# Layers written out, and the context tile's attention taken two head units at a time: one change to a two-layer fused transformer trunk

## The chip, the cores and the metric

The kernel runs on one core of a Trainium2 chip, as one launch. The time is device microseconds of that core, from the first to the last instruction of the program. The profiled execution is read through its profile page and through views of its trace; times inside it are microseconds from the start of the span unless marked ns.

## The reference

One inference step of a two-layer backbone over 256 latent tokens and 128 context tokens, which go through the kernel together as three tiles of 128 tokens: tiles 0 and 1 are latent, tile 2 is the context. Each layer normalises, projects, runs four mixers in parallel (A a bidirectional mLSTM, B neighbourhood attention, C sliding-window attention with a sink, D differential attention), gates and merges them, and then runs a grouped mixture of experts.

```python
for l in range(DEPTH):                                   # DEPTH = 2
    h = rmsnorm(x) * (1 + sc1) + sh1
    aq, ak, av, ao, ..., bq, bk, bv, cq, ck, cv, dq, dk, dv, gt = split(h @ w_in)
    # latent tokens attend latent keys (masked, biased) and cached context keys, in one softmax;
    # context tokens attend the 128 context keys only:
    s = einsum('bqhgd,bkhd->bhgqk', qx, k) * scale       # C: a sink logit joins the softmax
    p = softmax(s)                                       # D: p[:, :, 0] - lam * p[:, :, 1]
    y = einsum('bhgqk,bkhd->bqhgd', p, v)
    out = sum(sigmoid(gates) * (branches @ w_branch)) @ w_out
    x = x + g1 * out
    x = x + g2 * hier_moe(rmsnorm(x) * (1 + sc2) + sh2)
```

## The kernel before, in words

Every engine runs its own hand-written program, and semaphores join them. The body of a layer stands once in each engine's program, inside a hardware loop over the two layers (`Fori(0, DEPTH)`, L659 for SyncE, L790 for GpSimd, L944 for ScalarE, L1306 for TensorE, L1833 for VectorE). Since the layer number `l` is a register there, the number that a semaphore is waited for (`Signal.value`: layer times the count per layer, plus a constant) has to be worked out by register instructions. The expert part has a further hardware loop over its six tiles inside.

The order of work is one list, `SCHEDULE` (L109 to L214), that each engine walks. Its backbone is a row of GEMM units `("gemm", g)`: weights of 128x1024 numbers arrive in a ring `raw`, ScalarE rounds them to `whi`, GpSimd or VectorE subtracts to get `wlo`, and TensorE multiplies in three passes (`whi*hhi`, `wlo*hhi`, `whi*hlo`, L1328 to L1330) into the accumulator G: 18 products of 512 columns for a unit over the three token tiles. Other steps are put between units (`put`), or inside one, ahead of its second or third token tile (`put_inside`).

Attention is a pipeline of units `AU` (L91): (mixer, token tile, pair of heads). Each of the mixers B, C and D has 12 units, eight for the latent tiles and four for the context tile. Slot i of a mixer holds four steps: `sn` of unit i-1 (VectorE: reciprocal and scaling of the exponentials `prob`), `pv` of unit i-3 (TensorE: L1668 or L1671, probabilities by values into O; ScalarE and VectorE take O away as `bhi` and `blo`), `pt` of unit i-2 (TensorE transposes `prob` into T, L1641; ScalarE and VectorE copy it to `probT`), and `sc` of unit i (TensorE: scores into S, L1627, L1628 for latent tiles, L1630 for the context; VectorE: maximum, L2133; ScalarE: exponentials, L1171). Slots 0 to 8 stand after a GEMM unit each; slots 9 to 14, which hold most of the context tile's steps, stand half a unit apart:

```python
            if i < 9:
                put(g + i, *at)
            elif i % 2:
                put_inside(g + 9 + (i - 9) // 2, 1, *at)
            else:
                put(g + 9 + (i - 9) // 2, *at)
        return g + 12
```

The transposes of the next mixer's queries and keys (`tp`, L1546) use the same banks T0 and T1 as `pt` and are put inside units ahead of the third token tile. In the order rows below, `waits` lists the semaphores an instruction waits for: `pa_act` and `pb_dve` are the copies of the turned probabilities, `pn_dve` the scaled probabilities, `ol_dve` the values taken from O, `ex_act` the exponentials, `lo_done` a split weight unit, `ev_act` and `ev_dve` a GEMM tile taken out of G, `last_pe` and `sq_act` the end and the start of a layer.

Of the kernel before, what the change touches and what calls it, by code (L numbers as in the profile page):

```python
# [28 lines left out]
P = 128  # L29
D = 1024  # L30
# [60 lines left out]
AU = [(ty, t, j) for ty in "BCD" for t in range(TILES) for j in range(4)]  # L91
# [17 lines left out]
def schedule():  # L109
# [32 lines left out]
    def attention(g, first):  # L142
        for i in range(12 + 3):
            at = []
            if 1 <= i < 13:
# [3 lines left out]
            if 2 <= i < 14:  # L149
                at.append(("pt", first + i - 2))  # L150
            if i < 12:
# [17 lines left out]
    g = attention(g, 12)  # L169
# [3 lines left out]
    g = attention(g, 24)  # L173
# [25 lines left out]
    for g in range(NG):  # L199
# [3 lines left out]
        for t in range(1, TILES):  # L203
# [6 lines left out]
            (s[0] in ("sc", "sn", "pt", "pv") and s[1] >= 24)]  # L210
# [72 lines left out]
def program(nc, a, out, counts):  # L283

    ctx = ExitStack()
    with ctx:
# [73 lines left out]
        am = sb("am", [P, 2, 16])  # L360
# [286 lines left out]
        def _(sp):  # L647
# [11 lines left out]
            with sp.Fori(0, DEPTH) as l:  # L659
# [120 lines left out]
        def _(pool):  # L780
# [9 lines left out]
            with pool.Fori(0, DEPTH) as l:  # L790
# [144 lines left out]
        def _(act):  # L935
# [8 lines left out]
            with act.Fori(0, DEPTH) as l:  # L944
# [46 lines left out]
                for s in SCHEDULE:  # L991
# [109 lines left out]
                    elif s == ("dma", "gate1"):  # L1101
                        need(g_out, 0)
                        need(pv_pe, 23)
# [60 lines left out]
                    elif s[0] == "sc":  # L1164
# [3 lines left out]
                        w = 384 if t < 2 else 128  # L1168
                        for m in range(2):
                            src = prob[:, u % 2, m, 0:w] if u in BIASED else S[:, m, 0:w]  # L1170
                            e = nc.scalar.activation(prob[:, u % 2, m, 0:w], src, ACT.Exp,  # L1171
                                                     bias=am[:, u % 2, m:m + 1], accum_out=am[:, u % 2, 2 + m:3 + m])
                        if ty == "C":
                            e = nc.scalar.activation(am[:, u % 2, 6:8], am[:, u % 2, 4:6], ACT.Exp)
# [6 lines left out]
                        if u in (11, 23):  # L1181
                            act.wait_ge(*sc_pe.at(l, u))
                            load_keys(u // 12 + 1)
                    elif s[0] == "pt":
                        u = s[1]
                        w = 384 if AU[u][1] < 2 else 128
                        act.wait_ge(*pt_pe.at(l, u))
                        pa_act.of(nc.scalar.activation(probT[:, u % 2, 0, 0:w], T[:, 0, 0:w], ACT.Copy))
                    elif s[0] == "pv":
# [3 lines left out]
                        if ty == "D":  # L1193
                            yd_act.of(nc.scalar.activation(slot["Dq"][:, t, j * P:(j + 1) * P], O[:, 0:P], ACT.Copy))
                        else:
                            n = TYPES.index(ty)
                            if u == 12:
                                need(kv_out["B"], 1)
                                act.wait_ge(*rope_dve.at(l, 8))
                            oh_act.of(nc.scalar.activation(bhi[n][:, j, t * P:(t + 1) * P], O[:, 0:P], ACT.Copy))  # L1200
                        if u in (11, 23):
                            load_vals(u // 12 + 1)
# [76 lines left out]
        def _(pe):  # L1279
# [26 lines left out]
            with pe.Fori(0, DEPTH) as l:  # L1306
# [62 lines left out]
                for s in SCHEDULE:  # L1369
# [87 lines left out]
                    elif s[0] in ("gemm", "rest"):  # L1457
# [5 lines left out]
                        if i == 0 and kind == "branch":  # L1463
                            need(*((tl_dve, 3), (ol_dve, 11), (ol_dve, 23), (tl_dve, 7))[arg[0]])
# [149 lines left out]
                    elif s[0] == "sc":  # L1614
                        u = s[1]
                        ty, t, j = AU[u]
                        kj = j // 2 if ty == "C" else j
                        i = "BCD".index(ty)
                        need(tp_act, max(TP_NO[ty, "q", j], TP_NO[ty, "k", kj]))
                        if u % 12 == 0:  # L1620
                            need(keys_in, i)
                        free("S0", "S1")
                        for m in range(2):
                            r = slice(64 * m, 64 * m + 64)
                            q = qT[r, j, t * P:(t + 1) * P]
# [3 lines left out]
                            else:  # L1629
                                mm = nc.tensor.matmul(S[:, m, 0:128], q, kT[r, kj, 256:384], start=True, stop=True)  # L1630
                        sc_pe.of(mm)
                        read["S0"] = read["S1"] = (sa_dve, BIASED.index(u)) if u in BIASED else (ex_act, u)
                    elif s[0] == "pt":
# [5 lines left out]
                        for m in range(maps):  # L1639
                            for b in range(3 if t < 2 else 1):  # L1640
# [6 lines left out]
                    elif s[0] == "pv":  # L1647
# [5 lines left out]
                        if u % 12 == 0:  # L1653
                            need(vals_in, "BCD".index(ty))
                        free("O")
                        blocks = [0, 1, None] if t < 2 else [2]
# [6 lines left out]
                        for i, b in enumerate(blocks):  # L1663
# [764 lines left out]
```

## Time and profile before

| | |
|---|---|
| runs of the kernel before | 1719.42, 1721.44, 1723.40 us; median 1721.44 |
| the profiled execution | 1721.81 us, its span 1720.2 us |
| TensorE busy | 97% of the span |
| VectorE, ScalarE, GpSimd busy | 60%, 51%, 38% |
| mean granted TensorE clock | 0.995 |
| HBM | 341.71 MB read, 23.93 MB written |

The span is the time from the first to the last instruction; 1.6 us of the execution's time lie outside of it. A busy TensorE is not TensorE at its peak, since the ends of its products are modelled and they overlap; the loading of weights (PEld in the rows) shows more sharply when the array takes the next piece of work.

### The profile page before, as it was taken

To read this page: it belongs to the slowest core of one execution; us is meant where nothing else is said; L and a number is where in the kernel's file an instruction comes from. 1 tells how busy PE (TensorE), PEld (TensorE's weight loads), DVE (VectorE), ACT (ScalarE), POOL (GpSimd) and SP (SyncE) were. 2 spreads that over 40 slices of the span, in tenths; PEclk is the share of its full clock that TensorE was granted. 3 is DMA by queue.
4 is the path that set the end of the run, shared out by engine and by line. 5 is a ranking of instruction groups with operands and counts; after the bars stand their busy time and mean duration, and the time that the engine had idled before them with its cause. 6 is when DMAs were issued, how large, how long until landed. Compare 5 with 4: busy or idle time off the path is not lost.

```text
span 1720.2 us, 30904 instructions
## 1 busy us (share of the span) xinstructions
PE 1666.3 (97%) x10021; PEld 1332.3 (77%) x10021; DVE 1030.5 (60%) x1820; ACT 875.4 (51%) x1499; POOL 657.9 (38%) x414
## 2 busy tenths in 40 slices
PE   6999999999999999999989999999999999999997
PEld 5788787777888877777768888777778887777775
DVE  2226567564451179999860374775635413899997
ACT  2443344445443347788744334454445334587884
POOL 0545464334467621111125454543345775101102
PEclk8999999999999999999999999999999999999999
DMA  8833343254456559999965234334354653999994
GB/s 302 289 101 106 106 147 124 96 178 141 178 195 230 184 183 397 376 369 368 323 226 195 91 112 140 117 117 141 124 184 160 214 201 138 343 383 366 376 363 159
DMA packets 120849, 367.49 MB, mean 214 GB/s; under 512 B 11964, under 2 KB 34044, under 8 KB 120704
## 3 DMA queue, kind: packets, MB, share of 16 engines
q1 hardware_dynamic: 95024, 323.99, 52.3%
q0 software_dynamic: 6624, 24.18, 3.8%
q10 hardware_dynamic: 19056, 17.52, 3.3%
q8 instruction: 75, 1.23, 0.3%
q14 instruction: 70, 0.57, 0.1%
HBM read 341.71 MB, written 23.93 MB: 213 GB/s over the span
## 4 chain that ended last, share of the span: by engine, by line
PE 57%; issue 16%; DVE 13%; POOL 6%; ACT 5%; DMA 2%; SPq 1%; ACTq 0%; DVEq 0%; POOLq 0%
PE G L1328 15%; PE G L1330 13%; PE G L1329 13%; DVE wlo L1849 4%; POOL wlo L809 4%; ACT whi L970 2%; PE T L1641 2%; PE O L1385 2%; PE S L1627 2%; PE O L1671 1%; DVE pA L1849 1%; PE S L1328 1%; DMA pC<-in_units 1%; DVE pB L1849 1%; PE S L1330 1%
## 5 line engine op out<-in xcount | busy, mean ns | idle before, releaser
L809 POOL TENSOR_TENSOR wlo<-raw,whi 128x1024 fp32r<-128x1024 f32 x198 | 489.8, 2480 | 570.8 <-ACT whi L962 570.8
L1328 PE MATMUL G<-whi,hhi 128*128 128x512 f32 (+1 forms) x1440 | 579.4, 402 | 11.4 <-DVE wlo L1849 6.8
L1330 PE MATMUL G<-whi,hlo 128*128 128x512 f32 (+1 forms) x1440 | 558.1, 388 | 0.0
L1329 PE MATMUL G<-wlo,hhi 128*128 128x512 f32 (+1 forms) x1440 | 557.9, 387 | 0.0
L1328 PEld LDWEIGHTS G<-whi,hhi 128*128 128x128 f32 x1440 | 270.8, 188 | 90.6 <-DVE wlo L1849 16.6
L1330 PEld LDWEIGHTS G<-whi,hlo 128*128 128x128 f32 x1440 | 270.9, 188 | 57.6
L1329 PEld LDWEIGHTS G<-wlo,hhi 128*128 128x128 f32 x1440 | 271.5, 189 | 46.9
L962 ACT ACTIVATE whi<-raw 128x1024 fp32r<-128x1024 f32 x204 | 214.9, 1055 | 105.8 <-PE G L1330 71.2
L1849 DVE TENSOR_TENSOR wlo<-raw,whi 128x1024 fp32r<-128x1024 f32 x150 | 179.8, 1221 | 6.3 <-ACT whi L970 3.4
L970 ACT ACTIVATE whi<-raw 128x1024 fp32r<-128x1024 f32 x144 | 152.9, 1062 | 32.3 <-PE G L1330 18.0
L970 ACT ACTIVATE whi<-pA 128x1024 fp32r<-128x1024 f32 x72 | 76.6, 1063 | 41.7 <-PE G L1330 23.3
L1849 DVE TENSOR_TENSOR wlo<-pA,whi 128x1024 fp32r<-128x1024 f32 x72 | 88.0, 1224 | 15.8 <-ACT whi L970 14.0
L1171 ACT ACTIVATE prob<-prob,am 128x384 f32<-128x384 f32 x64 | 39.1, 612 | 110.7 <-DVE am L1849 59.6
L1849 DVE TENSOR_TENSOR wlo<-pB,whi 128x1024 fp32r<-128x1024 f32 x72 | 85.2, 1223 | 6.9 <-ACT whi L970 6.3
L1328 PE MATMUL S<-whi,ehi 128*128 128x512 f32 x192 | 79.4, 413 | 6.4 <-DVE elo L1849 6.3
L970 ACT ACTIVATE whi<-pB 128x1024 fp32r<-128x1024 f32 x72 | 75.2, 1058 | 10.6 <-PE G L1330 10.3
L1328 PE MATMUL G<-whi,bhi 128*128 128x512 f32 x192 | 79.2, 412 | 0.0
L1330 PE MATMUL S<-whi,elo 128*128 128x512 f32 x192 | 75.2, 392 | 0.0
L1330 PE MATMUL G<-whi,blo 128*128 128x512 f32 x192 | 75.1, 391 | 0.0
L1329 PE MATMUL S<-wlo,ehi 128*128 128x512 f32 x192 | 75.1, 391 | 0.0
L1329 PE MATMUL G<-wlo,bhi 128*128 128x512 f32 x192 | 74.9, 390 | 0.0
L804 POOL TENSOR_TENSOR sink_col<-ones 128x1 f32<-128x1 f32 x26 | 15.3, 587 | 149.6 <-ACT yo L1264 76.6
(383 smaller groups left out, 2385.7 us busy)
## 6 DMA issues: line engine op xcount, KB each, us to landing
raw<-in_units SPq DMA_DIRECT2D x426, 512.0 KB, 4.9
pA<-in_units SPq DMA_DIRECT2D x78, 512.0 KB, 6.1
pB<-in_units SPq DMA_DIRECT2D x72, 512.0 KB, 6.3
h_sorted<-sig POOLq DMA_DIRECT2D x12, 514.0 KB, 7.5
hs<-h_sorted POOLq DMA_DIRECT2D x10, 514.0 KB, 7.8
y_sorted<-yo POOLq DMA_DIRECT2D x10, 512.0 KB, 7.0
bias<-in_nat_bias ACTq DMA_DIRECT2D x16, 256.0 KB, 3.5
kT<-in_units SPq DMA_DIRECT2D x6, 512.0 KB, 5.0
```

Of the source, the lines that this page charges most:

```text
L809: lo_done.of(nc.gpsimd.tensor_tensor(wlo[:, k, :], raw[:, POS_OF[g] % RAW, :], whi[:, k, :].bitcast(F32), ALU.subtract))
L962: hi_done.of(nc.scalar.activation(whi[:, g % CONV, :], raw[:, p % RAW, :], ACT.Copy))
L970: hi_done.of(nc.scalar.activation(whi[:, n % CONV, :], expert_raw(n), ACT.Copy))
L1171: e = nc.scalar.activation(prob[:, u % 2, m, 0:w], src, ACT.Exp, bias=am[:, u % 2, m:m + 1], accum_out=am[:, u % 2, 2 + m:3 + m])
L1328: nc.tensor.matmul(dst, st_hi, mv_hi, start=start, stop=False)
L1329: nc.tensor.matmul(dst, st_hi, mv_lo, start=False, stop=False)
L1330: return nc.tensor.matmul(dst, st_lo, mv_hi, start=False, stop=stop)
L1385: mm = nc.tensor.matmul(O[32 * q:32 * q + 32, c0:c0 + P], cond[:, k, :], raw[:, MODPOS[j - MQ + 1 + q] % RAW, k * P:(k + 1) * P], start=(k ...
L1627: nc.tensor.matmul(S[:, m, 0:256], q, kT[r, kj, 0:256], start=True, stop=True)
L1641: mm = nc.tensor.transpose(T[:, m, b * P:(b + 1) * P], prob[:, u % 2, m, b * P:(b + 1) * P], ident[:, :])
L1671: mm = nc.tensor.matmul(O[64 * m:64 * m + 64, 0:P], values(b, lo, 64), pr, **fl)
L1849: return V.tensor_tensor(o, i0, i1, op)
```

## The change

It does three things. (1) In each engine's program the loop over the layers is a Python loop, so that the body of a layer stands twice and waits are against constants; the counting pass that precedes the build walks one layer. (2) A unit of the context tile covers two pairs of heads: a mixer has `NA` = 10 units instead of 12, and the last two put side by side in one step what were two steps' scores, exponentials, transposes and products. (3) The slots of B and C stand after one GEMM unit each, 13 of them, and the last one (the last `pv`) shares its place with the first slot of the next mixer. For D the last two of 13 slots stand inside and after one unit, so that D ends where it did.

```diff
-AU = [(ty, t, j) for ty in "BCD" for t in range(TILES) for j in range(4)]
+AU = [(ty, t, j) for ty in "BCD" for t in range(TILES) for j in (range(4) if t < 2 else (0, 2))]
+NA = len(AU) // 3
...
     def attention(g, first):
-        for i in range(12 + 3):
+        for i in range(NA + 3):
...
-            if i < 9:
+            if first < 2 * NA or i < NA + 1:
                 put(g + i, *at)
-            elif i % 2:
-                put_inside(g + 9 + (i - 9) // 2, 1, *at)
+            elif i == NA + 1:
+                put_inside(g + NA + 1, 1, *at)
             else:
-                put(g + 9 + (i - 9) // 2, *at)
-        return g + 12
+                put(g + NA + 1, *at)
+        return g + NA + 2
...
+    layers = DEPTH if counts else 1
...
-            with pe.Fori(0, DEPTH) as l:
+            for l in range(layers):
...
# ScalarE, exponentials: four of 128 columns instead of two in a context unit
-                        w = 384 if t < 2 else 128
-                        for m in range(2):
-                            src = prob[:, u % 2, m, 0:w] if u in BIASED else S[:, m, 0:w]
-                            e = nc.scalar.activation(prob[:, u % 2, m, 0:w], src, ACT.Exp,
-                                                     bias=am[:, u % 2, m:m + 1], accum_out=am[:, u % 2, 2 + m:3 + m])
+                        w, n = (384, 2) if t < 2 else (P, 4)
+                        for i in range(n):
+                            m, lo = i * 2 // n, i % (n // 2) * w
+                            src = prob[:, u % 2, m, lo:lo + w] if u in BIASED else S[:, m, lo:lo + w]
+                            e = nc.scalar.activation(prob[:, u % 2, m, lo:lo + w], src, ACT.Exp,
+                                                     bias=am[:, u % 2, i:i + 1], accum_out=am[:, u % 2, 4 + i:5 + i])
...
# TensorE, scores of a context unit: both pairs of heads side by side in S
-                        for m in range(2):
+                        for o, m in ((o, m) for o in range(len(pair)) for m in range(2)):
                             r = slice(64 * m, 64 * m + 64)
-                            q = qT[r, j, t * P:(t + 1) * P]
+                            q = qT[r, pair[o], t * P:(t + 1) * P]
...
-                                mm = nc.tensor.matmul(S[:, m, 0:128], q, kT[r, kj, 256:384], start=True, stop=True)
+                                mm = nc.tensor.matmul(S[:, m, o * P:(o + 1) * P], q, kT[r, kj, 256:384], start=True, stop=True)
...
# TensorE, transposes
-                            for b in range(3 if t < 2 else 1):
+                            for b in range(3 if t < 2 else 2):
...
# VectorE, scaling of a context unit (D adds the two maps in an operation of its own)
+                        both = both.rearrange("p m (j n) -> p m j n", j=2)
+                        scaled = tt(both, both, q[:, 20:24].rearrange("p (m j) -> p m j", m=2).unsqueeze(3)
+                                    .to_broadcast([P, 2, 2, P]), ALU.mult)
+                        if ty == "D":
+                            own(scaled)
+                            scaled = tt(both[:, 0], both[:, 0], both[:, 1], ALU.add)
+                        pn_dve.of(scaled)
```

The copies and the waits of the other engines follow the new units (widths of 256 instead of 128, `NA` in place of 12). The number of products, transposes and exponentials in a layer stays; only the grouping changes.

**First place: TensorE, mixer B of a layer, a step of the context tile.** Before, the step that holds the products, transposes and scores of one context unit each:

```order
L1313 REGISTER_ALU [waits pa_act]
L1671 MATMUL O<-probT,pB 64x128 [waits ol_dve,pb_dve]
L1671 MATMUL O<-probT,pB 64x128
L1641 MATMUL T<-ident,prob 128x128 [waits pn_dve]
L1641 MATMUL T<-ident,prob 128x128
L1313 REGISTER_ALU
L1630 MATMUL S<-kT,qT 128x128 [waits ex_act]
L1630 MATMUL S<-kT,qT 128x128
L1313 REGISTER_ALU
L1328 MATMUL G<-whi,bhi 128x512 [waits ev_act]
```

Now, the step in which the last latent unit's products meet the first context unit's transposes; no scores are left for it:

```order
L1680 MATMUL O<-probT,pB 64x128 [waits ol_dve]
L1680 MATMUL O<-probT,pB 64x128 x3
L1680 MATMUL O<-probT,vc 64x128 x2
L1649 MATMUL T<-ident,prob 128x128 [waits tp_act,pn_dve]
L1649 MATMUL T<-ident,prob 128x128 x3
L1335 MATMUL G<-whi,bhi 128x512 [waits lo_done]
```

The four transposes of two units stand in one piece, the scores have gone into the two steps ahead, and no register instruction stands between the pieces.

**Second place: TensorE, from mixer B to mixer C.** Now the last products of B and the first scores of C follow each other after one GEMM unit (before, they stood one unit apart):

```order
L1680 MATMUL O<-probT,pB 64x128 [waits ol_dve,pb_dve,pa_act]
L1680 MATMUL O<-probT,pB 64x128 x3
L1635 MATMUL S<-kT,qT 128x256 [waits ex_act,keys_in]
L1636 MATMUL S<-kT,qT 128x128
L1635 MATMUL S<-kT,qT 128x256
L1636 MATMUL S<-kT,qT 128x128
L1335 MATMUL G<-whi,hhi 128x512 [waits lo_done]
```

**Third place: GpSimd, from the first layer to the second.** Before, the loop's branch goes back to the body's start:

```order
L923 TENSOR_TENSOR sink_col<-ones 128x1 [waits last_pe]
L790 REGISTER_ALU
L790 COMPARE_AND_BRANCH
```

Now the second layer's first operations (the root of the mean square of each tile) follow in the same row of instructions:

```order
L926 TENSOR_TENSOR sink_col<-ones 128x1 [waits last_pe]
L817 TENSOR_TENSOR st<-st,cval 128x1 [waits sq_act,start_dve]
L821 TENSOR_TENSOR st<-st,cval 128x1 [waits pool_ord]
L817 TENSOR_TENSOR st<-st,cval 128x1 [waits sq_act]
L821 TENSOR_TENSOR st<-st,cval 128x1 [waits pool_ord]
```

The branch is gone there, on every engine; the branches of the expert loops stay and are now built once per layer.

## Rows read from the trace of the kernel before

**Rows 1.** The page, part 1: busy time and share of each engine.

```profile
PE 1666.3 (97%) x10021; PEld 1332.3 (77%) x10021; DVE 1030.5 (60%) x1820; ACT 875.4 (51%) x1499; POOL 657.9 (38%) x414
```

**Rows 2.** Windows: stretch, PE, PEld, DVE, ACT, POOL busy (x), clock, DMA share, GB/s.

```profile
246.00:492.00 246.00, 242.35 (x1707) 188.43 (x1708) 144.47 (x316) 119.96 (x309) 102.76 (x45) 1.00 0.42 143
636.00:866.00 230.00, 224.89 (x984) 173.21 (x983) 209.03 (x262) 174.46 (x210) 29.52 (x38) 1.00 0.95 357
```

**Rows 3.** Timeline, PEld, mixer B: start, us, line, load, xcount [idle before <-releaser].

```profile
315.34 0.19 PEld L1330 LDWEIGHTS G<-whi,blo 128*128 128x128 f32 x1
315.88 0.20 PEld L1671 LDWEIGHTS O<-probT,pB 128*64 128x64 f32 x4 [0.36 <-issue]
316.25 0.20 PEld L1641 LDWEIGHTS T<-ident,prob 128*128 128x128 f32 x2 [0.17 <-issue]
316.62 0.30 PEld L1630 LDWEIGHTS S<-kT,qT 64*128 64x128 f32 x4 [0.17 <-issue]
...
317.15 0.19 PEld L1329 LDWEIGHTS G<-wlo,bhi 128*128 128x128 f32 x1
317.38 0.19 PEld L1330 LDWEIGHTS G<-whi,blo 128*128 128x128 f32 x1
```

**Rows 4.** Timeline, PEld, mixer B: three more context steps, and six transposes together.

```profile
312.16 0.19 PEld L1330 LDWEIGHTS G<-whi,hlo 128*128 128x128 f32 x1
...
314.41 0.19 PEld L1329 LDWEIGHTS G<-wlo,bhi 128*128 128x128 f32 x1
...
323.76 0.19 PEld L1330 LDWEIGHTS G<-whi,blo 128*128 128x128 f32 x1
...
324.96 0.19 PEld L1329 LDWEIGHTS G<-wlo,bhi 128*128 128x128 f32 x1
...
1146.49 0.64 PEld L1641 LDWEIGHTS T<-ident,prob 128*128 128x128 f32 x6 [0.17 <-issue]
```

**Rows 5.** Timeline, PEld: a full latent step, and the first scores of mixer C.

```profile
289.33 0.19 PEld L1330 LDWEIGHTS G<-whi,hlo 128*128 128x128 f32 x1
...
292.45 0.19 PEld L1329 LDWEIGHTS G<-wlo,hhi 128*128 128x128 f32 x1
...
332.62 0.19 PEld L1330 LDWEIGHTS G<-whi,hlo 128*128 128x128 f32 x1
...
334.12 0.19 PEld L1329 LDWEIGHTS G<-wlo,hhi 128*128 128x128 f32 x1
```

**Rows 6.** Timeline, PEld, mixer D: a context step with scores, one without.

```profile
481.17 0.19 PEld L1330 LDWEIGHTS G<-whi,blo 128*128 128x128 f32 x1
...
482.57 0.19 PEld L1329 LDWEIGHTS G<-wlo,bhi 128*128 128x128 f32 x1
...
484.87 0.19 PEld L1330 LDWEIGHTS G<-whi,blo 128*128 128x128 f32 x1
...
485.66 0.19 PEld L1329 LDWEIGHTS G<-wlo,bhi 128*128 128x128 f32 x1
```

**Rows 7.** Waits of PEld, whole span (us in total, times, longest); one VectorE operation.

```profile
PEld T L1641 <- ACT qT L1133: 3.4, 6, 1.2
PEld T L1546 <- DVE probT L2162: 2.9, 2, 1.5
...
317.33 2.41 DVE L1849 TENSOR_TENSOR prob<-prob,am 128x256 f32<-128x256 f32 x1
```

**Rows 8.** Timeline at the end of the first layer, by engine; the last is an expert-loop row.

```profile
869.83 0.19 POOL L814 TENSOR_TENSOR st<-st,cval 128x1 f32<-128x1 f32 x1 [2.66 <-issue]
...
871.71 0.95 POOL L818 TENSOR_TENSOR st<-st,cval 128x1 f32<-128x1 f32 x1
...
869.61 1.06 ACT L1007 ACTIVATE sig<-pA 128x1024 f32<-128x1024 f32 x1 [1.31 <-DVE pA L1849]
...
871.50 0.75 DVE L1930 TENSOR_SCALAR pB<-pA,st 128x1024 f32<-128x1024 f32 x1 [1.92 <-POOL st L818]
...
873.58 0.65 PE L1349 MATMUL T<-ident,pB 128*128 128x128 f32 x4 [0.94 <-DVE pB L1930]
...
713.49 1.00 ACT L1264 ACTIVATE yo<-S 128x1024 f32<-128x1024 f32 x1
```

More of the change, by code:

```diff
@@ L168, in schedule @@
     put_inside(g - 1, 2, ("tp", "C", "k", 0), ("tp", "C", "k", 1))
-    g = attention(g, 12)
+    g = attention(g, NA)
     for i in range(4):
@@ L172, in schedule @@
         put_inside(g - 1 + i // 2, 2, ("tp", "D", "k", i))
-    g = attention(g, 24)
+    g = attention(g, 2 * NA)
     put(g, ("hn", 1))
@@ L789, in _ @@
             pool.memset(dummy[:, 11:12], 0.0).then_inc(yo_free.handle, 1)
-            with pool.Fori(0, DEPTH) as l:
+            for l in range(layers):
                 chain = [0]
@@ L943, in _ @@
             act.wait_ge(cond_dve, 2)
-            with act.Fori(0, DEPTH) as l:
+            for l in range(layers):
                 chain = [0]
@@ L1305, in _ @@
             pe.wait_ge(nx_dve.handle, 1)
-            with pe.Fori(0, DEPTH) as l:
+            for l in range(layers):
                 passed = {}
@@ L1832, in _ @@
             next_cols().then_inc(nx_dve.handle, 1)
-            with dve.Fori(0, DEPTH) as l:
+            for l in range(layers):
                 chain = [0]
@@ L2147, in _ @@
                         if ty == "C":
[L2148 to L2157 removed]
+                            own(tt(q[:, 4:4 + 2 * n], q[:, 4:4 + 2 * n], q[:, 12:12 + 2 * n], ALU.add))
@@ new lines, in _ @@
+                        own(V.reciprocal(q[:, 20:20 + 2 * n], q[:, 4:4 + 2 * n]))
+                        if ty == "D" and t < 2:
+                            own(V.tensor_scalar(prob[:, u % 2, 0, 0:w], prob[:, u % 2, 0, 0:w], q[:, 20:21], None, ALU.mult),
+                                V.tensor_scalar(q[:, 21:22], q[:, 21:22], lam[:, 5:6], None, ALU.mult))
+                            pn_dve.of(V.scalar_tensor_tensor(prob[:, u % 2, 0, 0:w], prob[:, u % 2, 1, 0:w], q[:, 21:22],
+                                                             prob[:, u % 2, 0, 0:w], ALU.mult, ALU.add))
+                            continue
@@ new lines, in _ @@
+                        if ty == "D":
+                            own(V.tensor_scalar(q[:, 22:24], q[:, 22:24], lam[:, 5:6], None, ALU.mult))
+                        both = prob[:, u % 2, :, 0:n * w]
+                        if n == 1:
+                            pn_dve.of(tt(both, both, q[:, 20:22].unsqueeze(2).to_broadcast([P, 2, w]), ALU.mult))
+                            continue
+                        both = both.rearrange("p m (j n) -> p m j n", j=2)
+                        scaled = tt(both, both, q[:, 20:24].rearrange("p (m j) -> p m j", m=2).unsqueeze(3)
+                                    .to_broadcast([P, 2, 2, P]), ALU.mult)
```

104 lines of the change are left out of this document (51 added, 53 removed).

## The prediction, made before the changed kernel was timed

> **What bounds the kernel now.** I read the busy shares first: TensorE is busy 97% of the span, the next engine 60% [rows 1]. Two stretches then say which engine a saving must come from. In the three mixers B, C and D of the first layer (246 to 492 us) TensorE has 242.4 of 246 us, VectorE and ScalarE under 150, DMA a share of 0.42, and the granted clock is 1.00 [rows 2]; only what takes the array less time makes this stretch shorter. In the experts (636 to 866 us) TensorE and the DMA (0.95) are both nearly full [rows 2]; the change leaves the work there as it is. A busy share of 97% leaves about 50 us idle, but it counts changeovers of the array as busy, so the weight loads must be read one by one. Between two GEMM products the loads start 0.23 us apart (317.15 and 317.38 [rows 3]). Where attention interrupts the GEMM, I take the step's price as the first GEMM load after it, less the last before it, less two paces (0.46): the product that was still running, and the one after. This holds streaming and changeovers together, as the array feels them.
>
> **Fewer, larger pieces.** Three context steps of mixer B stand in the rows:
>
> - products, transposes and scores of one unit each: 317.15 - 315.34 - 0.46 = 1.35 us [rows 3];
> - the same with twelve products instead of four: 314.41 - 312.16 - 0.46 = 1.79, so four more cost 0.22 [rows 4];
> - products and transposes alone: 324.96 - 323.76 - 0.46 = 0.74 [rows 4].
>
> So a piece of scores costs 1.35 - 0.74 = 0.61. Its four loads make two pairs, one to each half of the array, some 0.10 us a pair, so 0.20 is streaming; the row's 0.30 [rows 3] holds the last load too, and with 0.30 the term below would be 0.1 less for each piece. The rest, 0.41, is paid once for the piece whatever its size. A transpose is 0.11 ((0.64 - 0.20) / 4, [rows 3, 4]), so products and transposes stream 0.22 + 0.22, and 0.30 of their 0.74 is paid once for the interruption. Per mixer of kind B or C the change has the scores of the context in two pieces instead of four, and 13 interruptions instead of 15: 2 x 0.41 + 2 x 0.30 = 1.42 us.
>
> In D the step with scores costs 482.57 - 481.17 - 0.46 = 0.94, and without 485.66 - 484.87 - 0.46 = 0.33 [rows 6]. Two products and one transpose stream just that, so only the scores have a changeover: 0.61 - 0.20 = 0.41, twice, 0.82 per mixer. Products and transposes there have the shape of the GEMM's tiles (128 by 128), scores do not; that fits a changeover paid per change of tile shape.
>
> A layer saves 1.42 + 1.42 + 0.82 = 3.66 us, the two layers **7.3 us**. If the changeover of pieces twice as large were to grow with their size, nothing of this would be left; against it, the twelve products cost no more per load than four. Bounds: 5.5 (0.30 of each scores piece streams: 12 pieces fewer, 1.2 us less, and some of the 2 x 0.30 kept) to 8.5.
>
> **The shared place.** B's last products and C's first scores now interrupt the GEMM once. The full latent step (twelve products, six transposes, eight scores) costs 292.45 - 289.33 - 0.46 = 2.66 [rows 5]. Products and transposes of that size are 0.74 + 0.44 + 0.44 = 1.62, so the scores add 1.04, and C's first scores by themselves cost 334.12 - 332.62 - 0.46 = 1.04 [rows 5]. Joining two steps thus saves nothing that the rows show; I take 0.
>
> **The waits of the half-spaced steps.** With two steps in one unit the transposes come before ScalarE and VectorE have cleared T. TensorE's loads wait 3.4 us in 6 waits for ScalarE's `qT` copies, and 2.9 us in 2 for VectorE's copy `probT` [rows 7]. At 317.33 VectorE's scaling of one such unit takes 2.41 us [rows 7], with the next steps due half a unit (9 x 0.23 = 2.1 us) behind. Together 6.3 us. Some of that would have passed as a changeover anyway: 0.17 at each of 8 places, the gap where nothing is waited for [rows 3], so 4.9 go at most. With whole units between the steps (18 x 0.23 = 4.1 us) these waits should go. What is late next is ScalarE: a context unit now has four exponentials in a row, ahead of the turned keys' copies, and I let 0.5 us stay. The term is **4.4 us**, bounds 0 (each wait finds another late copy) and 4.9.
>
> Queued behind TensorE's last products in the shared place are the next mixer's scores and then the GEMM. Their wait is for VectorE's and ScalarE's copies of the transposes of one unit before, some 4 us earlier; work of that kind keeps up with the full latent step at the same spacing [rows 5], so I price it at nothing. Merged copies and scalings on VectorE and ScalarE lie beside TensorE, which has over 95 us more work than either in the stretch of 246 us [rows 2]: nothing too; if that cover went, one late copy would cost about what the single waits cost now, 1.2 to 1.5 us [rows 7].
>
> **The layer boundary.** GpSimd's first operation of layer 2 starts at 869.83 after 2.66 us in which it waited for nothing that the profile shows [rows 8]; the loop's branch is in that gap. Then the root ends at 871.71 + 0.95 = 872.66 for the last tile, VectorE normalises the first tile at 871.50, and TensorE's transposes start at 873.58 [rows 8]. Written out, GpSimd still can't finish before ScalarE: its activation ends at 869.61 + 1.06 = 870.67 [rows 8], and the root follows. Its own time of 0.95 us takes the chain to about 871.6 instead of 872.7. So of the 2.66 us, **1.1 us** lie on the path and the rest hides beside ScalarE. Bounds: 0.1 and 2.7.
>
> The Trainium skill (Advanced Engine Details and Errata, Control Flow Timing) gives about 108 ns for a compare-and-branch. By that price the boundary would be worth 0.1, and the sum would be 11.8 (1710.0 us); the idle 2.66 us of the row is far over it, and the measurement decides.
>
> **Register instructions.** The order shows one ahead of the scores and none ahead of L1641, yet both gaps are 0.17 us [rows 3]. Taken as 0, with bounds 0 and 8 (first rival).
>
> **The sum.** 7.3 + 4.4 + 1.1 = 12.8, and 1721.8 - 12.8 gives **1709.0 us** against the profiled execution, which lies 0.4 above the median of the runs; I do not correct for that. The expert part and all DMA traffic carry nothing: every transfer has the same size, and starts with its own GEMM unit. A mixer's GEMM units keep their number too, and D ends at the same unit.
>
> **Rivals.**
>
> *Register work is on TensorE's path.* Then each interruption loses part of its gap of 0.36 or 0.17 us [rows 3] when the constants come in. For: no engine is named as releaser, only "issue". Against: the equal gaps with and without a register instruction. With about 0.1 us off at each of some 80 remaining places it gives 8 us more: 1701. Chance 0.12.
>
> *The waits only move.* Four exponentials in a row and the joined mixers make ScalarE's or VectorE's copies late at the one-unit spacing, and the 4.4 us come back. For: VectorE's 2.41 us operation shows that a copy can be held up by another engine [rows 7]. Against: 18 products cover 4.1 us. Then 1721.8 - 7.3 - 1.1 + 1 = 1714. Chance 0.14.
>
> *Slower: the expert loops lose their place.* They stay hardware loops, but stand twice, at other addresses; a back edge that finds its target no longer at hand would idle its engine as GpSimd does at the layer boundary. Eight more such edges (four per layer beyond the first pass, TensorE's or the slowest engine's) at 2.7 us, less 0.3 that is there now, make 8 x 2.4 = 19, less the 12.8: 1728. It decides from about five such edges on. Against: the body of one expert tile is short beside a layer's, and ScalarE's first operation after such an edge has no idle time before it (the last row of [rows 8]); the body's length does not change. Chance 0.06.
> The Trainium skill (Runtime: NRT & Kernel Launch, on instruction fetch) says that a taken branch to a target outside the prefetched window of two pages has to fetch it by DMA; GpSimd's 2.66 us agree, and straight code would be fetched ahead.
>
> *The change does not do what it says.* The order shows fewer pieces, no register instructions, and no branch at the boundary; what is left is that the gaps do not follow the pieces (changeovers grow with size), and half of the waits stay: 1721.8 - 1.1 - 2.2 = 1718.5. Chance 0.06.
>
> **How the numbers follow.** The forecast has 0.62. Its own bounds (5.5 to 8.5, 0 to 4.9, 0.1 to 2.7) do not fall together; I take 1705 to 1713 for it. The range of 1700 to 1716.5 adds the first two rivals and leaves out the last two (0.12) and the far tail of the first. About 0.2% (3.4 us) is what a measurement of this kernel can tell from no change: faster means under 1718.0, slower over 1724.9. Faster: 0.62 + 0.12 + 0.14 less a little for mishaps, 0.86; within: 0.08, mostly the last rival; slower: 0.06.
>
> **What would show it.** In the trace after: a B or C context step of eight products and four transposes costs about 0.30 + 0.44 + 0.44 = 1.18 us, one of eight products and no transposes with eight scores of C about 1.8; no wait of TensorE for `probT` or `qT` ahead of its transposes; GpSimd's first operation of layer 2 without the 2.66 us; gaps of 0.17 and 0.36 us as before. I am wrong if these gaps shrink throughout (first rival), if waits for ScalarE or VectorE appear at the one-unit spacing (second), or if the experts take more than their 230 us (third).

## The result, and the profile after

| | before | after |
|---|---|---|
| median of 6 runs each | 1719.95 us (1717.42 to 1723.4) | 1704.19 us (1700.93 to 1706.39) |
| ratio, 95% interval | | 0.9906 [0.9896, 0.9917] |
| profiled execution, span | 1720.2 us | 1704.8 us |

The kernel is faster by 0.94%, 15.8 us between the medians, where 12.8 were forecast: inside the range and under its middle. It is 0.8 us below the narrower 1705 to 1713 that the prediction gave to its own account; the profiled execution, 1706.39 us, lies inside that. The busy shares say nothing of the gain (compare [rows 1]); neither do the windows of the two stretches [rows 2], in which TensorE is as full as before. The kernel is shorter mainly because the attention stretch ends earlier. Page, part 1, and windows (stretch, PE, PEld, DVE, ACT, POOL busy, clock, DMA share, GB/s) of the kernel after:

```profile
PE 1658.0 (97%) x10021; PEld 1333.3 (78%) x10021; DVE 1014.5 (60%) x1736; ACT 871.0 (51%) x1471; POOL 657.1 (39%) x414
```

```profile
240.00:484.00 244.00, 243.28 (x1753) 193.07 (x1754) 140.62 (x275) 119.58 (x298) 108.54 (x49) 1.00 0.42 144
627.00:857.00 230.00, 224.81 (x984) 173.10 (x984) 208.96 (x262) 174.31 (x210) 28.44 (x38) 1.00 0.95 357
...
868.00:871.50 3.50, 3.50 (x8) 2.75 (x9) 2.99 (x8) 2.00 (x3) 0.00 (x0) 0.50 0.79 273
```

Both kernels load the GEMM's weights in the same order, so the start of the same load can be read in every trace, and the span falls into stretches that compare. They are, in us, from one such load to the next (start: from the span's start to the ninth GEMM unit; A: from there to the start of a unit shortly ahead of B's first scores; attention: from there to past the end of D; to the boundary: up to a load within the experts, at 800.5 us before; boundary: the last expert tiles, the turn to layer 2 and its first eight units; then the same stretches of layer 2):

| kernel | start | A | attention 1 | to the boundary | boundary | A 2 | attention 2 | rest |
|---|---|---|---|---|---|---|---|---|
| before | 81.75 | 155.24 | 263.75 | 299.74 | 123.66 | 155.17 | 264.16 | 376.8 |
| before_again | 81.53 | 155.15 | 263.63 | 299.66 | 123.89 | 155.11 | 264.18 | 376.7 |
| after | 81.12 | 154.72 | 256.29 | 299.19 | 125.59 | 154.72 | 256.71 | 376.5 |
| after_again | 79.87 | 154.72 | 256.31 | 299.40 | 124.58 | 154.72 | 257.23 | 376.5 |
| layers_only | 79.06 | 154.75 | 262.98 | 299.46 | 125.00 | 154.77 | 263.11 | 376.9 |
| attention_only | 79.39 | 155.27 | 257.75 | 299.65 | 123.97 | 155.13 | 257.01 | 376.9 |
| merged_half | 77.50 | 154.72 | 260.47 | 299.43 | 125.14 | 154.75 | 260.35 | 376.5 |
| pt_first | 79.90 | 154.77 | 256.38 | 299.42 | 125.13 | 154.71 | 257.73 | 376.5 |
| busy | 80.41 | 154.73 | 256.35 | 299.45 | 125.41 | 154.75 | 256.32 | 376.6 |
| best | 83.25 | 154.73 | 254.53 | 299.27 | 124.61 | 154.75 | 254.79 | 376.7 |
| best_busy2 | 79.95 | 154.76 | 254.83 | 299.19 | 123.52 | 154.74 | 254.70 | 376.6 |
| layers_pe | 80.16 | 155.09 | 264.16 | 299.69 | 125.41 | 155.11 | 263.83 | 377.0 |
| layers_act_dve | 82.79 | 154.79 | 262.99 | 299.21 | 125.32 | 154.81 | 262.87 | 376.7 |
| apart | 78.51 | 154.71 | 257.79 | 299.16 | 124.91 | 154.71 | 257.87 | 376.5 |

The stretches A and attention repeat within 0.6 us from trace to trace, most of them within 0.1; the start does not (77.5 to 83.3). Of the 15.4 us between the two spans, 7.5 are in each attention stretch, 0.5 in each stretch A, 0.6 in the start, 0.8 in the remainder, and the boundary gives 1.9 back.

The pieces on TensorE's loads came out as the sum had them. Timeline of the kernel after, PEld, mixer B (start, us, line, load, count, [idle before <-releaser]):

```profile
315.81 0.19 PEld L1337 LDWEIGHTS G<-whi,blo 128*128 128x128 f32 x1
316.36 0.42 PEld L1680 LDWEIGHTS O<-probT,pB 128*64 128x64 f32 x8 [0.36 <-issue]
316.75 0.25 PEld L1680 LDWEIGHTS O<-probT,vc 128*64 128x64 f32 x4
317.17 0.42 PEld L1649 LDWEIGHTS T<-ident,prob 128*128 128x128 f32 x4 [0.17 <-issue]
317.56 0.19 PEld L1335 LDWEIGHTS G<-whi,bhi 128*128 128x128 f32 x1
317.67 0.19 PEld L1336 LDWEIGHTS G<-wlo,bhi 128*128 128x128 f32 x1
...
322.02 0.19 PEld L1337 LDWEIGHTS G<-whi,blo 128*128 128x128 f32 x1
322.57 0.42 PEld L1680 LDWEIGHTS O<-probT,pB 128*64 128x64 f32 x8 [0.36 <-issue]
323.16 0.42 PEld L1649 LDWEIGHTS T<-ident,prob 128*128 128x128 f32 x4 [0.17 <-issue]
...
323.66 0.19 PEld L1336 LDWEIGHTS G<-wlo,hhi 128*128 128x128 f32 x1
...
327.34 0.19 PEld L1337 LDWEIGHTS G<-whi,hlo 128*128 128x128 f32 x1
327.88 0.42 PEld L1680 LDWEIGHTS O<-probT,pB 128*64 128x64 f32 x8 [0.35 <-issue]
328.47 0.31 PEld L1635 LDWEIGHTS S<-kT,qT 64*128 64x128 f32 x4 [0.17 <-issue]
...
329.44 0.19 PEld L1336 LDWEIGHTS G<-wlo,hhi 128*128 128x128 f32 x1
```

Twice as many transposes as in [rows 3], and the gaps ahead of the pieces are still 0.36 and 0.17. The second step costs 323.66 - 322.02 - 0.46 = 1.18, as forecast. (The prediction called the load it counts to the first after the interruption. It is the second, as here 317.67, and the two paces are right for that one.) The waits of [rows 7] for `qT` and `probT` are gone. Waits of PEld after (us in total, times, longest), and of the changed kernel's second trace, after_again:

```profile
PEld O L1680 <- issue: 14.6, 40, 0.5
...
PEld T L1649 <- issue: 7.9, 38, 0.7
...
PEld T L1649 <- issue: 8.6, 38, 1.1
```

Of the 38 gaps ahead of the transposes, 35 are the changeover of 0.17. Three are longer: 0.74 and 0.69, which the kernel before has too (0.71 and 0.72), and in layer 2 one of 0.44, which is 1.06 in after_again. That last one stands in the step of B right behind the turned queries of C, so one step at the one-unit spacing is still late.

### The profile page after: what moved, and what is told of

The parts are those of the page before. It is cut to its first block, busy times and chain, and to the rows that moved or that the text cites. A ratio compares the mean times of both kernels' runs of the same rounds, so it can differ in the third digit from the quotient of the medians.

```text
span 1704.8 us, 27109 instructions
## 1 busy us (share of the span) xinstructions
PE 1658.0 (97%) x10021; PEld 1333.3 (78%) x10021; DVE 1014.5 (60%) x1736; ACT 871.0 (51%) x1471; POOL 657.1 (39%) x414
## 4 chain that ended last, share of the span: by engine, by line
PE 71%; DVE 14%; issue 5%; ACT 4%; DMA 3%; POOL 1%; SPq 1%; ACTq 0%; DVEq 0%; POOLq 0%
PE G L1335 18%; PE G L1337 17%; PE G L1336 17%; DVE wlo L1858 6%; ACT whi L973 3%; DVE pA L1858 2%; PE T L1649 2%; PE O L1392 2%; DMA x_scratch<-pA 2%; PE S L1635 1%; PE O L1680 1%; PE S L1335 1%; DVE prob L1858 1%; PE S L1337 1%; PE S L1336 1%
## 5 line engine op out<-in xcount | busy, mean ns | idle before, releaser
L807 POOL TENSOR_TENSOR sink_col<-ones 128x1 f32<-128x1 f32 x26 | 15.4, 592 | 149.4 <-ACT yo L1271 76.7
```

## The experiments

### The parts of the change alone

**layers_only**: the kernel before, with the layer loops written out.

```diff
-            with pe.Fori(0, DEPTH) as l:
+            for l in range(layers):
```

(the same on the other four engines, and one layer in the counting pass). Expected:

> The kernel before with the layers written out on all five engines and nothing else changed. My account: register instructions hide behind the array, so the attention stretch (about 270 us from B's first scores to D's last products) keeps its length within 0.3 us per layer and the gaps of 0.36 and 0.17 us stay. At the boundary GpSimd's 2.66 us go, but in the changed kernel the clock of TensorE then fell to 0.50 for some 3.6 us, which costs 1.8 us; so the total is within 0 to 1.5 us of the kernel before, ratio 0.999 to 1.001. Rival (register work is on TensorE's path): each layer's attention stretch is 2 us or more shorter, ratio 0.997 or less. Rival of the prediction as made (boundary worth 1.1 us, no clock effect): ratio 0.9994, and the first products of layer 2 at a pace of 0.23 us.

Measured: 1716.89 us, ratio 0.9971 [0.9960, 0.9982]. None of the three accounts given beforehand fits. Of the 4.2 us between the profiled spans 2.7 are in the start, which varies from trace to trace; the other stretches give 1.5 in all. The gaps of TensorE's loads are unchanged, yet stretch A is 0.4 to 0.5 us shorter and attention 0.8 and 1.1. The gain sits where TensorE waits for VectorE or ScalarE to clear a tile; in stretch A it is all at one place, where 1.53 us from one load to the next became 0.98. Before (PEld, two places), then written out, the same places:

```profile
175.46 0.19 PEld L1328 LDWEIGHTS G<-whi,hhi 128*128 128x128 f32 x1 [0.72 <-ACT pB L1074]
...
252.48 0.64 PEld L1680 LDWEIGHTS T<-ident,pA 128*128 128x128 f32 x6 [0.82 <-DVE pA L1849]
```

```profile
172.21 0.19 PEld L1330 LDWEIGHTS G<-whi,hhi 128*128 128x128 f32 x1 [0.17 <-POOL wlo L811]
...
248.86 0.64 PEld L1682 LDWEIGHTS T<-ident,pA 128*128 128x128 f32 x6 [0.40 <-DVE pA L1851]
```

The boundary is 1.3 us longer instead of 1.1 shorter, and the clock falls there as in the changed kernel (below).

**attention_only**: the changed kernel with `Fori` back on SyncE, GpSimd, TensorE and VectorE. ScalarE's layers stay written out.

> The changed kernel with the hardware loop over the layers kept on four engines (ScalarE's layers stay written out). My account: the attention parts carry all of the gain, about 7.4 us in each layer, and the boundary keeps the clock at 1.00 since the identity products are again stretched by the branch: ratio 0.9900 to 0.9915, that is at least as fast as the changed kernel. Rival (writing out the layers gives a share of the gain through register work): ratio 0.993 or more.

Measured: 1706.80 us, 0.9914 [0.9900, 0.9929]. The attention part carries most of the gain, as my account said. As a time this kernel can't be told from the changed one (0.9906 [0.9896, 0.9917]). By its stretches it is not as fast: attention is 1.5 and 0.3 us longer, A 0.6 and 0.4. Of the 1.5 us, 1.0 is a wait in layer 1 at the step behind the turned queries, the same step as above (timeline, PEld):

```profile
309.95 0.64 PEld L1649 LDWEIGHTS T<-ident,prob 128*128 128x128 f32 x6 [1.20 <-issue]
```

The boundary is short (123.97) and the clock stays up.

**layers_pe** and **layers_act_dve**: the loop written out on TensorE alone, and on ScalarE and VectorE alone.

> The kernel before with TensorE's layers alone written out. My account: nothing is gained inside the layers, since TensorE's register instructions hide; at the boundary TensorE no longer loses 2.08 us to its branch, so its identity products end earlier, it idles about 3.7 us before the transposes (GpSimd's branch is still there) and the clock falls: 1.8 us lost, ratio 1.000 to 1.002. Rival (TensorE's register work is what the written-out layers save): ratio 0.998 or less.

> The kernel before with ScalarE's and VectorE's layers alone written out. My account: their register instructions stand in chains that TensorE waits for (0.55 us at one wait for ScalarE's pB, 0.42 at one for VectorE's pA, 0.35 ahead of the experts, some smaller ones), so about 1.3 to 1.6 us per layer go, and TensorE's clock stays 1.00 at the boundary: ratio 0.9975 to 0.9985. Rival: 1.000, all of it comes with TensorE's or GpSimd's own loop.

Measured: 1722.00 us, 1.0010 [1.0001, 1.0019], and 1720.86 us, 1.0001 [0.9992, 1.0010]. TensorE's own register instructions show no gain in the layers (A is 155.09 and 155.11 us, attention 264.16 and 263.83, all within 0.4 us of the kernel before), and without its branch the boundary is 1.5 to 1.8 us longer. ScalarE's and VectorE's alone give A and attention the length that they have in layers_only (154.79, 262.99, 262.87). Since attention_only has ScalarE written out too and its stretch A is that of the kernel before (155.27), A needs VectorE written out; whether VectorE alone would do was not run. For the attention stretch the runs tell only that it is the two engines together. My sum for this kernel was right within the layers and wrong as a total: the trace has a start 1.0 us later, and early in layer 2 a wait of TensorE that the kernel before does not have:

```profile
896.25 0.19 PEld L1330 LDWEIGHTS G<-whi,hhi 128*128 128x128 f32 x1 [1.45 <-DVE hlo L1851]
```

Its cause wasn't followed further.

**merged_half**: the changed kernel with the old half-unit spacing of the steps from 9 on in B and C.

```diff
+            if first < 2 * NA and i >= 9:
+                if i % 2:
+                    put_inside(g + 9 + (i - 9) // 2, 1, *at)
+                else:
+                    put(g + 9 + (i - 9) // 2, *at)
```

> The changed kernel with the old half-unit spacing for the steps 9 to 12 of B and C (merged units, the mixer ends half a unit before the next one begins, so no shared place). My account: fewer pieces still save about 3.7 us per layer, and the waits for copies of ScalarE and VectorE ahead of the transposes come back, 2 to 4 us per layer, now with longer copies and four exponentials: ratio 0.993 to 0.996. Rival (spacing is not what makes the waits; merging them removes them): as the changed kernel, 0.9906.

Measured: 1711.71 us, 0.9949 [0.9936, 0.9961], inside the range of my account. Attention is 4.2 and 3.6 us longer than in the changed kernel, and the waits are there, one of them under a name and two under none (timeline, PEld):

```profile
309.47 0.42 PEld L1654 LDWEIGHTS T<-ident,prob 128*128 128x128 f32 x4 [0.84 <-issue]
...
315.51 0.31 PEld L1558 LDWEIGHTS T<-ident,pC 128*128 128x128 f32 x3 [1.34 <-DVE probT L2188]
...
394.14 0.42 PEld L1654 LDWEIGHTS T<-ident,prob 128*128 128x128 f32 x4 [1.84 <-issue]
```

Where nothing is waited for this gap is 0.17, so "issue" hides 0.7 and 1.7 us of waiting here. Merging alone is worth 2.5 to 2.8 us per layer (262.98 - 260.47 and 263.11 - 260.35), less than the pieces save, since the waits grew. Spacing is worth another 3.6 to 4.2, with about 0.4 of it from the two shared places that come with it.

**apart**: the shared place undone; B's and C's last products stand inside the next unit.

```diff
+            if first < 2 * NA and i == NA + 2:
+                put_inside(g + i, 1, *at)
```

> The changed kernel with the shared place undone: the last products of B and of C stand inside the next GEMM unit, ahead of its second token tile, half a unit before or after what they shared with. In the trace of the changed kernel the shared step costs 1.64 us, where products alone would be 0.78 and scores alone 1.05, so sharing saves 0.19 at each of 4 places: 0.8 us slower than the changed kernel (ratio 0.991). By the prediction as made it saves nothing: ratio as the changed kernel.

Measured: 1705.73 us, 0.9918 [0.9905, 0.9932]. The changed kernel had 1704.14 us beside it (after_again), and the intervals overlap, so the stretches have to tell. In B the products alone cost 0.79 and C's scores 1.05, together 1.84 against 1.64 in one place: sharing saves 0.20. Most of the rest of the 1.2 to 1.5 us per layer is 1.1 us in C, where the products now stand right ahead of the modulation's products in the same bank O, and these start after 1.20 us where they otherwise do after 0.36:

```profile
404.38 0.42 PEld L1682 LDWEIGHTS O<-probT,pC 128*64 128x64 f32 x8 [0.36 <-issue]
406.00 1.72 PEld L1394 LDWEIGHTS O<-raw,cond 128*32 128x32 f32 x64 [1.20 <-issue]
```

### What a changeover is

**pt_first**: the changed kernel with the transposes ahead of the products in every step.

```diff
+            if 2 <= i < NA + 2:
+                at.append(("pt", first + i - 2))
             if i >= 3:
                 at.append(("pv", first + i - 3))
-            if 2 <= i < NA + 2:
-                at.append(("pt", first + i - 2))
```

> The changed kernel with the transposes ahead of the products in every step (transposes, products, scores instead of products, transposes, scores); same instructions. If a changeover is paid where the shape of the array's tiles changes, the change from the GEMM to the transposes is free (both 128 by 128), and one of four changeovers of a B or C step goes: about 0.2 to 0.35 us at each of some 20 steps per layer, 8 to 14 us in all less what late copies give back, ratio 0.983 to 0.988. If instead each piece pays for its start whatever its shape, nothing changes: 0.9906.

Measured: 1703.54 us, 0.9892 [0.9877, 0.9907]. The total can't be told from the changed kernel's. The order matters, but less than expected. A full step (timeline, PEld):

```profile
279.53 0.19 PEld L1337 LDWEIGHTS G<-whi,hlo 128*128 128x128 f32 x1
279.75 0.81 PEld L1649 LDWEIGHTS T<-ident,prob 128*128 128x128 f32 x6
280.73 0.42 PEld L1680 LDWEIGHTS O<-probT,pB 128*64 128x64 f32 x8 [0.17 <-issue]
...
281.53 0.31 PEld L1635 LDWEIGHTS S<-kT,qT 64*128 64x128 f32 x4 [0.17 <-issue]
...
282.50 0.19 PEld L1336 LDWEIGHTS G<-wlo,hhi 128*128 128x128 f32 x1
...
307.73 0.64 PEld L1649 LDWEIGHTS T<-ident,prob 128*128 128x128 f32 x6 [0.99 <-issue]
```

From the GEMM to the transposes, both 128 by 128, there is no gap (279.53 + 0.22 = 279.75); the gaps stand where the shape changes. The step costs 2.51 instead of 2.66: 0.15 saved and not the whole gap of 0.35, since the six loads of the transposes now take 0.81 us instead of 0.64. The last row shows what took the gain back: a step right behind turned queries has its transposes wait for T (0.99 us; in the other order the products stand in that time). In D, where products and transposes have one shape, the step is 2.05 either way.

The Trainium skill (TensorEngine Tiling (Array Packing), Key Properties) says that a change of tiling mode drains TensorE. The trace agrees: 0.35 us from the GEMM to a piece with 64 rows or columns, 0.17 between pieces of different shape, none between equal shapes. No run here shows more of the mechanism than these gaps.

**best**: transposes first in steps 3 to 8 only, and the longer row of identity products of the next experiment.

> As the kernel before this one, and in steps 3 to 8 of every mixer the transposes stand ahead of the products (in later steps, where turned queries and keys have just used T0 and T1, the products stay first). The experiment with the transposes first everywhere had 0.15 us less at each full step of B and C, and gave 0.6 and 1.0 us back at the one step per mixer that follows turned queries. So 12 steps per layer, 24 x 0.15 = 3.6 us less than the kernel before this one: ratio 0.9868 to 0.9880. If the 0.15 us is taken back by something later, 0.9890 to 0.9900.

Measured: 1699.84 us, 0.9875 [0.9860, 0.9890]. Attention is 254.53 and 254.79, 1.8 and 1.9 us under the changed kernel: the expected 3.6 us in all.

### The boundary

With the branch gone, TensorE's identity products (`keep_busy`, which compute nothing that is used) run in one row, TensorE idles 2.59 us, and the first nine products of layer 2 start 0.43 us apart instead of 0.23. Timeline of PE after:

```profile
857.70 3.73 PE L1373 MATMUL S<-ident 128*128 128x128 f32 x32
...
864.02 0.85 PE L1356 MATMUL T<-ident,pB 128*128 128x128 f32 x6 [2.59 <-ACT pB L1028]
...
867.94 0.80 PE L1335 MATMUL G<-whi,hhi 128*128 128x512 f32 x1 [1.97 <-DVE wlo L1858]
868.53 0.63 PE L1336 MATMUL G<-wlo,hhi 128*128 128x512 f32 x1
868.96 0.63 PE L1337 MATMUL G<-whi,hlo 128*128 128x512 f32 x1
```

The granted clock is 0.50 there (the last window above), the 1.2 GHz level. The first 18 products take 5.78 us from start to start instead of 3.98: 1.8 us lost, and 1.6 to 1.9 in the other traces in which the clock fell.

**busy**: 20 more passes in that idle time, ahead of the transposes.

```diff
-                            keep_busy(S[:, 0, 0:P], BUSY_BEGIN)
+                            keep_busy(S[:, 0, 0:P], BUSY_BEGIN if l == 0 else 16)
```

> The changed kernel with 20 more passes of the identity product (ten more products, 0.117 us a pass, 2.3 us) ahead of the second layer's first transposes, nothing else. If the granted clock fell to 0.50 because TensorE had idled 2.59 us between the identity products and the transposes, the clock now stays 1.00 over the first products of layer 2, these start 0.23 us apart instead of 0.43, and the time falls by about 1.8 us against the changed kernel (ratio to before 0.9890 to 0.9900). If the fall has another cause (the 2 us of idle time behind the transposes, which were there before too), the pace stays 0.43 and the ratio 0.9906.

Measured: 1702.97 us, 0.9894 [0.9879, 0.9909], which can't be told from the changed kernel. The trace decides for the second of the two outcomes: the row of identity products is longer, the idle time before the transposes 0.37, and the clock falls all the same.

```profile
857.35 5.97 PE L1373 MATMUL S<-ident 128*128 128x128 f32 x52
863.68 0.85 PE L1356 MATMUL T<-ident,pB 128*128 128x128 f32 x6 [0.37 <-ACT pB L1028]
...
867.60 0.50 PE L1335 MATMUL G<-whi,hhi 128*128 128x512 f32 x1 [2.42 <-DVE wlo L1858]
...
868.67 0.63 PE L1335 MATMUL G<-whi,hhi 128*128 128x512 f32 x1
```

**best_busy2**: as best, with 18 passes more behind the transposes.

```diff
+                        if not w and l:
+                            keep_busy(G[:, 1, 0:P], 9)
```

> The kernel with transposes ahead of products in steps 3 to 8 and ten more identity products at the boundary, and now nine more (18 passes, 2.1 us) behind the second layer's first transposes, where TensorE idled 2.4 us. In the trace without them the clock still fell to 0.5 over the first products of layer 2. If idle time behind the transposes is what is left of the cause, the clock stays 1.00 there and 1.3 to 1.8 us go: ratio 0.986 to 0.987. If the clock falls for what TensorE does before, or by chance of the execution, the pace is 0.43 again and the ratio that of the kernel without them, 0.9875.

Measured: 1700.04 us, 0.9889 [0.9874, 0.9904]. The clock stays at 1.00, and the first 18 products take 1.6 us less than in best. The boundary is 123.52 instead of 124.61, since 0.5 us came back in a later wait for ScalarE's `pA`:

```profile
862.12 0.82 PE L1356 MATMUL S<-ident,pB 128*128 128x128 f32 x6
862.77 2.17 PE L1373 MATMUL G<-ident 128*128 128x128 f32 x18
865.36 0.50 PE L1335 MATMUL G<-whi,hhi 128*128 128x512 f32 x1 [0.41 <-DVE wlo L1860]
865.69 0.39 PE L1336 MATMUL G<-wlo,hhi 128*128 128x512 f32 x1
```

The ratio is over the 0.986 to 0.987 expected, and as a time it can't be told from best (both near 1700); the gain is shown in the trace alone. Against the changed kernel best is clearly faster (0.9875 [0.9860, 0.9890] beside 0.9906 [0.9896, 0.9917]); best_busy2 had 1700.04 beside the 1704.14 of after_again, with intervals that overlap.

**after_again** and **before_again**: both kernels once more.

> The changed kernel once more, beside the two others: ratio 0.9895 to 0.9917 as measured before. Its trace tells whether the clock falls to 0.50 at the second layer's first products every time (then about 1.8 us of layer 2's start are the change's own doing) or in some executions.

> The kernel before once more, one look. If the clock over the first products of layer 2 is 1.00 again, its absence in the kernel before is no chance; if it falls, the 1.8 us that the changed kernel seems to lose there are in both kernels' medians and no cost of the change. The attention stretch should be the same as in the first trace within 0.3 us.

Measured: 1704.14 us, 0.9905 [0.9890, 0.9920]; and a single execution of 1721.47 us. The clock falls again in the one and not in the other. Over all fourteen traces it never fell in the four where TensorE's own loop branch splits the identity products (before twice, attention_only, layers_act_dve), and it fell in nine of the ten others, all but best_busy2. In layers_pe nothing but TensorE's loop was changed, and the clock fell. So in these traces it is TensorE's branch that kept the clock up. Whether it falls in every execution of the changed kernel they can't say: the six runs of the result go from 1700.93 us at a mean clock of 0.998 to 1706.39 at 0.993.

Why the branch matters is open. Before, the same 2.43 us of idle time stood ahead of the first product (its chain begins with the transposes at 873.58 [rows 8]), and another 2.08 and 0.94 us besides, more than in busy. Nor does the fall follow one particular idle time. In the changed kernel the clock was down before the 1.97 us ahead of the first product were over (its mean is 0.62 from 864 to 868), while in busy it was 1.00 from 864 to 867.60. So best_busy2 shows only that filling the second idle time helps in a kernel where the first is filled too.

## Why the prediction was right, and where it was not

The sum was 12.8 us and the measurement 15.8 (15.4 between the profiled spans). By its own terms:

- **Fewer, larger pieces, 7.3 us.** Measured 7.8: in B and C (as steps without a wait) 10.67 us of steps (from the first context scores to the next mixer's first scores) became 9.12, saving 1.55 each where 1.42 stood, and D's 6.43 became 5.64, saving 0.79 where 0.82 stood. The difference is the shared place, priced at nothing and worth 0.2 each time. The split of a piece into a fixed part and streaming held to 0.02: eight loads of scores cost 0.83 where four cost 0.61.
- **The waits of the half-spaced steps, 4.4 us.** Undersized. Attention is 6.7 and 6.4 us shorter than in layers_only; less 3.9 for the pieces, 2.8 and 2.5 are left for the waits, 5.3 in all. Four waits make 4.6 of it, priced as the prediction prices steps: 1.30 and 1.34 at the transposes of C's queries, 0.99 and 1.00 at a late step of C. The allowance of 0.5 us for ScalarE's four exponentials was not needed. And 0.17 was taken off at all 8 places, where the two turnings of queries have the GEMM's shape and start after 0.04 when nothing is waited for; with 0.04 there the bound is 5.2 instead of 4.9.
- **The layer boundary, 1.1 us.** Wrong in sign: the stretch is 1.9 us longer. GpSimd's 2.66 us of idle time did go, and its last root ends 1.0 us earlier, counted from the start of the identity products (5.09 instead of 6.10 us). But ScalarE's normalised tile `pB`, begun 5.04 us after that start now and 5.05 before, then came last, so that layer 2's first GEMM product is only 0.7 us earlier (10.24 instead of 10.97 us). The same edit took TensorE's branch out of its row of identity products, and the fallen clock cost 1.8 us. Another 0.7 us is a longer wait for ScalarE's `pA` some units later (second fence); it varies as much between traces of kernels that share this edit, so that it can't be laid to the change. The step that failed is the one that followed the chain through GpSimd, VectorE and ScalarE and never asked what the branch did to TensorE, the engine that bounds. Timeline of POOL and ACT after, where [rows 8] had the gap:

```profile
857.95 0.35 POOL L926 TENSOR_TENSOR sink_col<-ones 128x1 f32<-128x1 f32 x1 [19.95 <-PE O L1794]
858.26 0.19 POOL L817 TENSOR_TENSOR st<-st,cval 128x1 f32<-128x1 f32 x1
...
862.24 0.55 POOL L821 TENSOR_TENSOR st<-st,cval 128x1 f32<-128x1 f32 x1
...
862.74 1.13 ACT L1028 ACTIVATE pB<-pA,st 128x1024 f32<-128x1024 f32 x1
```

The wait for `pA`, PE, before and after:

```profile
900.52 0.50 PE L1328 MATMUL G<-whi,hhi 128*128 128x512 f32 x1 [0.67 <-ACT pA L1074]
...
893.36 0.47 PE L1335 MATMUL G<-whi,hhi 128*128 128x512 f32 x1 [1.39 <-ACT pA L1077]
```

- **Register instructions, 0.** Right for TensorE, where the argument was from equal gaps and layers_pe confirms it; wrong as a total. About 3 us (layers_only against before: 0.5 and 0.4 in A, 0.8 and 1.1 in attention, 0.3 up to the boundary) come from VectorE's and ScalarE's, which stand in chains that TensorE waits for. The prediction costed the engine that bounds and not those it waits for.
- **The experts' loops.** The third rival did not happen: 224.81 of 230 us busy after, 224.89 before, and the stretch to the boundary is no longer.
- **The first and second rivals.** Register work on TensorE's path is excluded by the unchanged gaps. The waits mostly went and did not move, with one exception: the step of B behind the turned queries of C. Its transposes waited already before in layer 2 (0.39) and still do (0.44, and 1.06 in after_again). So the second rival holds for one step in a layer, at up to 0.9 us.

Two errors of about 3 us, the boundary against the forecast and the registers for it, cancelled. That is luck: the total is better than its parts. The start of the span, which the change hardly touches, varies by up to 5.8 us between traces of all kernels (77.5 to 83.3), at least in part with the clock: over the first 60 us the mean granted clock is 0.97 in merged_half, the shortest start, and 0.88 in best, the longest. So differences of 1 to 2 us between medians of four runs, as between best and best_busy2, are not evidence here; the stretches are.

## What to carry to other kernels

Price each interruption of a saturated TensorE as a fixed changeover plus streaming, from the starts of the loads on both sides; the fixed part is paid where the shape of the array's tiles changes, so group small pieces, and put pieces of the GEMM's own shape next to the GEMM. A stretch bounded by TensorE was still 0.4 to 1.1 us longer here by the register work of the engines that clear its banks, so cost those too. An idle time put down to "issue" can be a wait: compare it with the smallest gap of the same kind. When a stall is removed beside products that only keep the clock up, look at the granted clock after it.

## What was not expected of the hardware

- The clock at layer 2's first products fell to 0.50 after an unbroken row of identity products of 3.73 or 5.97 us, and stayed at 1.00 after 2.39 us of them, 2.08 us of pause and 1.60 more. More work ahead of the transposes (busy) did not prevent it; work in the idle time behind them (best_busy2) did.
- A step's price fell by 0.15 us for turning the order of two pieces alone (2.66 to 2.51).
